# Stacked real and imaginary factors in the long convolution's DFT steps, and a new split of the projection's half chunks between two stretches

## The reference

```python
proj = rms_norm(x, norm1) @ w_in           # 1024 -> [x0 | x1 | v of 512 each | q | k | v]
x0, x1, v = split(short_conv(hy_in))       # centred width-3 taps
u = x1 * v
U = rfft(u, n=2 * L, axis=1)               # L = 2048 or 256
K = rfft(concat([h_f, 0, reversed(h_b)]))  # from a small MLP over positions
y = irfft(U * K, n=2 * L)[:, :L] + u * hy_skip
y_hy = x0 * y
```

## Time and profile before

| | us |
|---|---|
| median of 3 runs | 2774.67 |
| lowest, highest | 2774.14, 2776.64 |
| the profiled execution | 2775.71 |
| its span, first to last instruction | 2773.9 |
| busy in the span: PE, DVE, ACT, POOL | 2677.5, 2167.6, 1370.8, 1254.7 |
| input's transform | 451 to 545 |
| spectrum | 553 to 736 |

### The profile page before, as it was taken

How to read it: one execution, slowest core, us unless ns; L and a number is a source line. 1 busy time by engine, 2 the same in 40 slices (tenths; PEclk the granted TensorE clock), 3 DMA queues, 4 the chain that set the end, 5 groups by cost and what they waited for, 6 DMA issues and landing times.

```text
span 2773.9 us, 39326 instructions
## 1 busy us (share of the span) xinstructions
PE 2677.5 (97%) x13969; PEld 2429.0 (88%) x13969; DVE 2167.6 (78%) x2474; ACT 1370.8 (49%) x2333; POOL 1254.7 (45%) x1168
## 2 busy tenths in 40 slices
PE   8999899999998999998999999999999989999998
PEld 6878798888887888887999999899999989999997
DVE  6765666777667778776788888888888898888887
ACT  5564554545446877774434343534334353434342
POOL 3545211133211444456677774445555444443443
PEclk9999999999999999999999999999999999999999
DMA  7688998887698346444544443554443355333332
GB/s 236 210 291 265 300 252 242 267 235 203 194 284 215 113 122 157 128 125 141 168 143 135 142 128 93 185 160 115 115 116 107 91 174 165 89 90 92 91 88 88
DMA packets 464858, 454.42 MB, mean 164 GB/s; under 512 B 51854, under 2 KB 374030, under 8 KB 464375
## 3 DMA queue, kind: packets, MB, share of 16 engines
q1 hardware_dynamic: 435096, 371.54, 46.5%
q0 software_dynamic: 29568, 80.36, 9.0%
HBM read 329.63 MB, written 122.18 MB: 163 GB/s over the span
## 4 chain that ended last, share of the span: by engine, by line
PE 84%; DVE 6%; DMA 4%; issue 2%; ACT 1%; POOL 1%; SPq 1%; DVEq 0%; ACTq 0%; POOLq 0%
PE ff_banks L85 17%; PE ff_banks L86 17%; PE ff_banks L87 17%; PE pr_acc L85 4%; PE pr_acc L86 4%; PE pr_acc L87 4%; PE pr_gen L85 3%; PE pr_gen L87 2%; PE pr_gen L86 2%; PE am_mix L85 2%; PE am_mix L87 2%; PE am_mix L86 2%; PE am_turn L2164 2%; DMA xkeep_dram<-pr_xs 1%; PE am_acc L2178 1%
## 5 line engine op out<-in xcount | busy, mean ns | idle before, releaser
L3283 DVE TENSOR_TENSOR ff_h<-ff_h,ff_banks 128x1536 f32<-128x1536 f32 x231 | 402.8, 1744 | 6.3 <-PE ff_banks L87 5.5
L3119 ACT COPY ff_r<-ff_banks 128x384 f32<-128x384 f32 x198 | 94.9, 479 | 592.5 <-PE ff_banks L87 592.4
L3266 DVE TENSOR_TENSOR ff_dlo<-ff_dlo_raw,ff_dhi 128x512 fp32r<-128x512 f32 x231 | 210.0, 909 | 175.0 <-ACT ff_dhi L3149 174.9
L85 PE MATMUL ff_banks<-ff_xhi,ff_ghi 128*128 128x384 f32 x924 | 314.6, 340 | 14.3 <-DVE ff_silu L3243 6.5
L85 PE MATMUL pr_acc<-pr_xhi,pr_whi 128*128 128x386 f32 (+1 forms) x864 | 304.1, 352 | 11.1 <-DVE pr_xlo L1525 11.1
L87 PE MATMUL ff_banks<-ff_xhi,ff_glo 128*128 128x384 f32 x924 | 312.6, 338 | 0.0
L86 PE MATMUL ff_banks<-ff_xlo,ff_ghi 128*128 128x384 f32 x924 | 312.2, 338 | 0.0
L85 PE MATMUL ff_banks<-ff_xhi,ff_uhi 128*128 128x384 f32 x924 | 310.8, 336 | 0.8 <-ACT ff_r L3119 0.6
L86 PE MATMUL ff_banks<-ff_xlo,ff_uhi 128*128 128x384 f32 x924 | 310.6, 336 | 0.0
L87 PE MATMUL ff_banks<-ff_xhi,ff_ulo 128*128 128x384 f32 x924 | 310.0, 335 | 0.0
L2975 POOL TENSOR_TENSOR ff_act<-ff_act,ff_silu 128x384 f32<-128x384 f32 x99 | 116.8, 1179 | 417.9 <-issue 235.5
(11 more groups left out here) (316 smaller groups left out, 6926.0 us busy)
## 6 DMA issues: line engine op xcount, KB each, us to landing
ff_glo_raw<-w_gate_up SPq DMA_DIRECT2D x132, 256.0 KB, 3.0
ff_ulo_raw<-w_gate_up SPq DMA_DIRECT2D x132, 256.0 KB, 3.0
ff_dlo_raw<-dsum_dram SPq DMA_DIRECT2D x132, 256.0 KB, 2.7
pr_raw<-w_in SPq DMA_DIRECT2D x108, 256.0 KB, 6.1
ff_dlo_raw<-w_down SPq DMA_DIRECT2D x99, 256.0 KB, 2.6
f_dram<-fi_out POOLq DMA_DIRECT2D x32, 512.0 KB, 5.3
fs_a<-f_dram SPq DMA_DIRECT2D x32, 512.0 KB, 8.3
pr_xs<-x SPq DMA_DIRECT2D x18, 512.0 KB, 6.8
```

Source lines behind the costliest of these rows:

```text
L85: pe.matmul(out, still[0], moving[0], start=start, stop=False, skip_group_check=goes_on)
L3119: act.copy(kept[n][:], bank(X)).then_inc(copied, 1)
L3266: dve.tensor_tensor(dlo[d_slot(n)][:], din[d_slot(n)][:], dhi[d_slot(n)][:].bitcast(F32), ALU.subtract).then_inc(d_low, 1)
L3283: dve.tensor_tensor(to, to, lowered_all(k), ALU.add).then_inc(added, 1)
```

## The change

- **Stacking.** The real and the imaginary part of 64 rows each are put one above the other in one tile of 128 rows (`quads`): rows 0 to 63 one part, rows 64 to 127 the other, in two halves c. A new table (`g4`, built on POOL out of `dft16` into the place of `pr_g16`: 2 DMAs, 8 small copies) does the complex 16-point DFT of such a tile in one triple. So a step's forward product takes 2 triples instead of 4, and so does its return.
- **Crossing.** The complex product needs each part against the other one too. ACT copies rows 64 to 127 of `pr_gen` into rows 0 to 63 of `sp_crossed` with a factor of -1, and rows 0 to 63 into rows 64 to 127: four copies of 64x512 a step. DVE multiplies `pr_gen` (two instructions, 128x512) and `sp_crossed` (one, 128x1024) with two spectra: one holds the real part in both halves of the rows, the other the imaginary part. So `sp_k` is loaded twice as often, 512 KB each; POOL adds instead of subtracting and adding.
- **DMAs in quarters.** Loads of `sp_a` and `sp_k` (j at least 2) and stores to `z_dram` are four DMAs each, to or from 64 partitions, runs of 2 KB instead of 4 KB.
- **Slots.** `sp_a` and `sp_k` have three slots; `sp_alo` lies on the place of `sp_a` (the low part overwrites the octet); `sp_yf` has two slots and lies on the place of `sp_ylo`. With that POOL's sum of step j waits for the return of step j - 2.
- **Order.** A step's octet is split in the step itself (from j = 0 on) behind the products, formerly a step later ahead of them; POOL stores z of step j - 4 ahead of the sum.
- **Half chunks.** The input's transform has three half chunks to two steps instead of four (8 fewer in all), the spectrum five to two steps instead of four for j below 18 (9 more in all).

The diff, cut to its core:

```diff
+    def quads(rows8, c):
+        return rows8.rearrange("(n h k) x -> h n k x", h=2, k=4)[c]
+    def spectrum(j, imaginary=0):
+        return j if j < 2 else 2 * j - 2 + imaginary
+    def products(j):
+        return 2 * min(j, 2) + 3 * max(j - 2, 0)
...
         for t in range(N2):
             u_step(t)
             yield
-            yield
+            if t % 2:
+                yield
         for j in range(NJ + 2):
             if j < NJ:
                 product_step(j)
             yield
             return_step(j - 2)
             yield
+            if j % 2 and j < NJ:
+                yield
...
@@ product_step of sync @@
         def product_step(j):
             if j == 0:
-                bring_octet(0)
-                bring_octet(1)
-            elif 2 <= j < NOCT:
-                bring_octet(j)
+                for t in range(3):
+                    bring_octet(t)
+                return
+            if 2 <= j < NJ - 1:
+                bring_k(spectrum(j + 1))
+            if 2 <= j < NOCT - 1:
+                bring_octet(j + 1)
+            if j < NJ - 1:
+                bring_k(spectrum(j + 1, 1))
...
@@ bring_k of sync, bring_octet alike @@
+            for c in range(2):
+                for d in range(2):
+                    sp.dma_start(hk[64 * d:64 * d + 64, u % 3, c], quads(k_dram[t], c)[:, :, o:o + HY]).then_inc(hk_in[u % 3], 16)
...
@@ product_step of gpsimd @@
+            if j >= 4:
+                store_z(j - 4)
+            pool.wait_ge(product, products(j + 1))
+            if j >= 2:
+                pool.wait_ge(returned, 2 * j - 2)
+                for c in range(2):
+                    pool.tensor_tensor(yf[:, j % 2, c, :], pa[:, c, :], pb[:, c, :], ALU.add).then_inc(y_summed, 1)
+                return
...
@@ product_step of tensor, j from 2, then return_step @@
+                pe.wait_ge(product, products(j))
+                for c in range(2):
+                    triple(pe, gen[:, c, :], (g16[:, 0, 0], g16[:, 0, 1]), (ahi[:, j % 2, c], alo[:, (j - 2) % 3, c]), True, True).then_inc(h_spectral, 1)
+                return
...
-                        m, q = (((0, 0), (1, 1)), ((2, 0), (0, 1)))[c][n]
-                        last = triple(pe, gen[:, 2 + c, :], (g16[:, m, 0], g16[:, m, 1]), (yhi[:, j % 2, q], ylo[:, j % 2, q]), n == 0, n == 1)
+                    last = triple(pe, gen[:, 2 + c, :], (g16[:, 1, 0], g16[:, 1, 1]), (yhi[:, j % 2, c], ylo[:, j % 2, c]), True, True)
...
@@ product_step of scalar @@
         def product_step(j):
+            if j >= 2:
+                for c in range(2):
+                    act.wait_ge(h_spectral, 2 * j + 1 + c)
+                    act.wait_ge(product, products(j) + c)
+                    act.activation(crossed[0:64, c], gen[64:128, c, :], ACT.Copy, scale=-1.0).then_inc(swapped, 1)
+                    act.copy(crossed[64:128, c], gen[0:64, c, :]).then_inc(swapped, 1)
+            if j < NOCT:
+                octet_high(j)
             if j:
                 y_part(j - 1)
-            if 1 <= j < NJ - 1:
-                octet_high(j - 1)
...
@@ product_step of vector, j from 2 @@
+                u, v = spectrum(j), spectrum(j, 1)
+                dve.wait_ge(h_spectral, 2 * j + 2)
+                for c in (1, 0):
+                    if c == 0:
+                        dve.wait_ge(swapped, 4 * j - 6)
+                    dve.tensor_tensor(pa[:, c], hk[:, u % 3, c], gen[:, c, :], ALU.mult).then_inc(product, 1)
+                dve.wait_ge(swapped, 4 * j - 4)
+                dve.wait_ge(hk_in[v % 3], spectrum_in(v))
+                dve.tensor_tensor(pb[:], hk[:, v % 3], crossed[:], ALU.mult).then_inc(product, 1)
+            if j < NOCT:
+                octet_low(j)
+            if j:
+                y_part(j - 1)
```

134 lines of the change are left out of this document (81 added, 53 removed).

## The result

After the change the kernel takes **2785.66 us** in the median of 4 runs (2782.12 to 2790.39), before 2774.40 (2774.13 to 2776.64) beside it: ratio 1.0042, 95% interval 1.0030 to 1.0054. It is slower by 11 us, where 2763 and "faster" had been forecast. The time lies inside the range and near the price of rival 1, but the trace does not show rival 1's mechanism.

What follows compares the result with a forecast made beforehand. PE was taken as the bound, busy 2677.5 of 2773.9 us. From 2775.7, less 44.3 for matmuls, plus losses of 10, 10, 8, 2 and 2, less 1.0, came 2762, given as 2763 us; range 2742 to 2792.

Steps and rivals of the forecast that it cites:

- rival 1: Spectrum stretch: DMA engines become the bound, with loads into 64 partitions too slow; slower, priced at 2787 us; chance 0.27.
- PE: what goes: 192 matmuls leave the forward products and returns of 16 spectrum steps: 44.3 us gained if nothing else waits.
- PE: what moves: 8 half chunks leave the input's transform and 9 join the spectrum; by itself this costs PE nothing.
- The terms for the edge and for u loads: End of the input's transform loses 10 us (4 to 16); u loads with less time to land, 2 us (0 to 6).
- The first piece: At the end of the input's transform PE waits 6 us for u loads queued behind SP's store of k.
- The second piece: At the transform's end the chunks' way out of PSUM stands behind the first octet on ACT: 8 us more.
- Events 66 to 71: Round 4's split of x beside the first octets, with less PE time to hide under: 8 us (3 to 15) lost.
- DVE in the spectrum: DVE takes 9.7 us a step beside q units, 0.9 over PE; loss 10 us (5 to 18).
- ACT and POOL: Spectrum steps: ACT busy 7.7 of 9.7 us, POOL's sum done about 4.6 us after the products, hidden; counted as nothing.
- SP's queue: Spectrum step has 12 issues, 6 to 7 us plus 1.5 of 9.7; the second spectrum fits by 1 to 2 us.
- Rival 3: Spectrum loop from DVE over SP's queue, landing at 9 us, gives 11.5 us a step: no change, 2774; chance 0.10.
- What would show it: Spectrum: DMA share near 1, PE 85 to 90%, q steps 9.5 to 10 us, PE idle 14 us, 192 fewer matmuls.

Runs made afterwards that it cites:

- d3: n1 with the spectrum loads after the third half, POOL's sums (zeros written instead) and ACT's crossing copies all left out; 2747.6 us, ratio 0.9908.
- e4: The changed kernel with ACT and DVE splitting the first octet in step 1 instead of step 0; 2787.0 us, ratio 1.0045.
- e1: The changed kernel with the half chunks back where they were before, so the stacking alone; 2774.0 us, ratio 0.9995.
- m1: n1 with POOL writing zeros in place of its sums; 2763.1 us, ratio 0.9961.
- s1: n1 with the sum made by DVE at the end of its step instead of by POOL; 2767.9 us, ratio 0.9978.
- s2: The changed kernel, still 12 issues, with the sum made by DVE instead of POOL; 2778.5 us, ratio 1.0018.
- e3: The changed kernel with POOL issuing the real spectrum's loads from step 3 on, leaving SP 8 issues a step; 2780.9 us, ratio 1.0026.
- n2: The changed kernel with k and a laid out so that SP makes 5 load issues a step instead of 12; 2781.4 us, ratio 1.0027.
- t1: s1 with DVE's low part of y moved into its wait for the crossing, and ACT's high part ahead of the crossing copies; 2761.2 us, ratio 0.9952.
- e2: The kernel before with only the half chunks moved, no stacking; 2790.2 us, ratio 1.0056.
- t2: t1 with the half chunks moved as in the changed kernel; 2774.0 us, ratio 0.9999.
- k1: The stacking alone with each spectrum half and octet brought by one load, 3 issues a step, halves with leading dimension 2; 3007.4 us, ratio 1.0831.
- n1: The stacking alone with a spectrum half as two plain loads and an octet as one, 5 issues a step instead of 12; 2776.3 us, ratio 1.0014.

## Why the prediction was wrong, step by step

- **PE: what goes.** Right in number. The 44.3 us stood under "if nothing else waits", but the clock had no term: with a granted clock of 0.91 in place of 1.00 PE's half chunks took 359 ns a matmul in the spectrum where they took 339 (means of L85 into `pr_acc`), and the whole run's busy time fell by 33.8 only. In the sum of costs this is the largest missing term, some 18 us in the two stretches by the estimate above; the waits themselves came to 38 us where 32 of loss had been forecast. No run holds the clock fixed, but where the waits go (d3) it is back at 0.99.
- **PE: what moves.** "This costs PE nothing by itself" failed. The half chunks cost 12 to 16 us over the same kernel without the move in three of four pairs. The terms for the edge and for u loads (12 us) came near what the transform lost (14.6), in part by luck. The first piece was right with its mechanism: PE stood 7.50 us (forecast 6) for a load of u that SP issued at 536.20, behind the store of k and six loads of the spectrum. The second piece, 8 us for the blocked ACT, was mislaid: with it taken away (e4) nothing came back. The 3 to 8 us of the inverse transform had no term, and the price of the low clock after the stop (12 matmuls by 0.20 more, 2.5 us) none either. Above all, this sum of costs was never set against the question what the move brings: without it (e1) the kernel was no slower than before.
- **Events 66 to 71.** The 8 us priced for them came out: PE waited 10.6 us for the low part of x in the spectrum where it had waited 1.3. The prediction looked for an idle PE in two pieces around the first product; the second piece is this one, 30 us after it.
- **DVE in the spectrum.** This is the step whose cost failed. It had 9.7 us to a step and 10 us of loss. The changed kernel took 10.95 in the mean of the last 12 steps (products from 604.5 to 735.9), 11.8 in the step shown, and PE waited 17.6 us for DVE's products, beside which its clock fell. The 9.2 us of work left out that the low parts now start beside POOL's sums (+1.08 for y in every step, as much for the weights in 4 of 10). The trace of before had the pair, seen from POOL's side: 2.19 in place of 1.28. The prediction turned it into "4.6 us from the products' end", asked only when POOL would be done, and never what the same overlap does to DVE. The crossing was priced at 0.5 and measured 0.73, near enough. Without POOL's sums (m1) the stacked kernel is 13 us faster, with DVE making them itself (s1, s2) 7 to 8.
- **ACT and POOL: "I count nothing."** The term that failed, as above. POOL's two sums took 4.4 us (4.6 forecast) and hid; their price was on DVE.
- **SP's queue.** "It fits by 1 to 2 us" failed, by less: 0.59 us an issue was right, but 12 of them are 7.1 and not "6 to 7", and back to back four take 2.5, so 7.4. In the window shown the queue has no gap, over the whole spectrum SP itself waited 36 us for others, most of it for DVE; DVE waited 7.5 us in all in three waits for a spectrum half. Repaired (e3, n2), it is worth 4 to 5 us in the change, at the edge of the noise, and nothing in the median of e1.
- **Rival 1.** Its price of 2787 met the time for another reason. Landing stayed at 3.1 us where it should have grown, the share was 0.81 in the stretch, and t1 moved 287 to 290 GB/s with all its spectra going through 64 partitions at a time, where the rival needed 225 or less (by the prediction's own sum it is slower than before from 238 down). What the prediction took from the Trainium skill, SBUF — State Buffer, section "Can I just issue two DMAs to hit both halves?", that a second load for the other half adds only 6%, does not describe these loads. The DMA engines may be the next limit behind DVE: m1 and t1 reach shares of 1.06 and 1.08 in 600 to 640.
- **Rival 3** named the loop over SP and its break-even of 11.6 us; the change came near it (10.95), with the edge on top, but through DVE's work and not through landing at 9 us.
- **What would show it.** PE in the spectrum at 85% (forecast 85 to 90) and 192 fewer matmuls were right; steps of 9.5 to 10 us and a DMA share near 1 were not.

What stays open: all that makes the inverse transform 7 to 8 us longer when the half chunks shift. A part is bookkeeping: from the last product on, PE has 13 to 18 matmuls more to do there (593 to 609 from e1 to the change, 624 to 637 from before to e2, 595 to 613 from t1 to t2), some 3 us. PE's idle time there grows by 2 to 5 us (in the change 3.5 for a table and 2.5 for a low part of z), and the rest is slower matmuls (granted clock 0.96 in place of 0.99 in the change and e2). No run isolates one of the waits.

## What to carry to other kernels

When work is taken from the engine that sets the time, write down the queue of the next engine as a whole step, instruction behind instruction, and take each duration from a row in which the same neighbours run; an overlap of two engines that slows one of them has to be priced for the other too. Price the matmuls beside short waits too: here the slower clock cost PE about half as much again as the waits. When repairs are worth 5 to 13 us in 2770, compare medians of ten executions and not stretches of one trace; here the two readings gave 9 and 28 us for the same three edits. Filler work that covers waits is not free to move: ask what it covered where it stood.

## What the runs showed of the hardware

- **DVE and POOL hold each other off whole.** The low part of y, two inputs in SBUF, took 1.22 us in all 16 cases of before and 2.31 in all 14 of the change between 570 and 722; POOL's sum took 1.28 alone, 2.2 in turn. Who starts first keeps its time: the low part of a, which starts just ahead of the sum (653.95 against 654.11), stays at 1.22. In m1 POOL only writes, and the low parts took 1.22; this does not test writing beside them, since the two writes (0.99 us from 640.82 on) are over when the low part of y starts (641.82). By the Trainium skill, SBUF — State Buffer, section "Who interferes with whom", a DVE instruction with two SBUF inputs contends with a GpSimd instruction that reads SBUF, and whoever issues first holds the port for its whole instruction; the rows agree for two reading instructions, and the rule would have given the missing stretch of DVE's low parts.
- **A load whose outer dimension is 2 moves 49 GB/s** in whole slices of k1, and holds up SP's queue behind it: single issues took 9 to 11 us in its spectrum.
- **An issue on SP costs about the same for 128, 256 and 512 KB** where it goes to 64 partitions or has a split row (0.59, 0.60 and 0.55 to 0.60 us in the change and n1), so the count of issues is what a full queue feels. A plain load of 256 KB (`ur_us`) took 0.33 in the median.
- **After a stop of 7.5 us** the next twelve matmuls came 0.43 us apart at a granted clock of 0.50, three more 0.32 apart, and then it was 1.00 again.
